# First attention of a two-layer kernel: keys laid out over all 128 partitions, one masked maximum for all scores, and two output strips begun before the attention ends

## The reference, cut to what matters

```python
# q (512 tokens, 8 heads, 64); k, v (512, 2 key heads, 64); k_ctx, v_ctx (256, 2, 64)
s_ctx = q . k_ctx * 64**-0.5            # all 256 context keys
s_loc = q . k     * 64**-0.5            # only keys with |i - j| <= 128
p = softmax(concat([sink, s_ctx, s_loc]))
att = p_ctx @ v_ctx + p_loc @ v         # four query heads share one key head
x = x + gate * (concat([att, conv]) @ w_out)
```

## Time and profile before

| | |
|---|---|
| median of 3 runs | 2669.1 us (2667.86 to 2671.85) |
| the profiled execution | 2669.28 us, its span 2667.3 us |
| PE busy | 2558.0 us (96%) |
| DVE busy | 1161.4 us (44%) |
| ACT busy | 752.9 us (28%) |
| TensorE clock granted, mean | 0.967 |
| first attention | 189.6 to 310.8 us |

### The profile page before, as it was taken

How to read it: one execution, slowest core, us unless ns; L and a number is a source line. 1 busy time by engine, 2 the same in 40 slices (tenths; PEclk the granted TensorE clock), 3 DMA queues, 4 the chain that set the end, 5 groups by cost and what they waited for, 6 DMA issues and landing times.

```text
span 2667.3 us, 29296 instructions
## 1 busy us (share of the span) xinstructions
PE 2558.0 (96%) x10842; PEld 1792.7 (67%) x10842; DVE 1161.4 (44%) x1793; ACT 752.9 (28%) x1052; POOL 29.4 (1%) x24
## 2 busy tenths in 40 slices
PE   6989969999999699999999999999999999999999
PEld 2765533333333488888988888888887566888887
DVE  5765351222221644443644443444435456544432
ACT  3124331000010423322433322333223435433321
POOL 0000000000000300000000000000000000000000
PEclk9986889999999799999899999999999999999999
DMA  6650138999999223331232322333322120323322
GB/s 243 199 188 1 55 151 345 422 422 421 422 422 377 79 88 101 101 109 59 88 95 97 108 98 83 95 98 98 113 92 76 59 72 9 95 95 97 108 98 75
DMA packets 80858, 403.58 MB, mean 151 GB/s; under 512 B 8984, under 2 KB 9496, under 8 KB 55968
## 3 DMA queue, kind: packets, MB, share of 16 engines
q1 hardware_dynamic: 80800, 402.82, 41.3%
HBM read 400.69 MB, written 2.10 MB: 151 GB/s over the span
## 4 chain that ended last, share of the span: by engine, by line
PE 88%; DVE 5%; DMA 2%; ACT 2%; issue 2%; POOL 0%; SPq 0%; DVEq 0%; ACTq 0%; POOLq 0%
PE pb L945 21%; PE pb L947 21%; PE pb L946 21%; PE pb L1150 8%; PE pb L1176 4%; PE pb L1137 2%; PE pb L1116 2%; DMA stage<-in_w_in 1%; PE pb L1038 1%; PE pb L1051 1%; PE pb L1065 1%; DMA adaw<-in_w_ada 1%; PE pb L1461 1%; PE pb L1331 1%; PE pb L1039 1%
## 5 line engine op out<-in xcount | busy, mean ns | idle before, releaser
L1485 DVE TENSOR_TENSOR wL<-stage,wH 128x1024 fp32r<-128x1024 f32 (+2 forms) x303 | 392.7, 1297 | 838.1 <-ACT wH L554 837.8
L945 PE MATMUL pb<-hH,wH 128*128 128x512 f32 x1688 | 668.7, 396 | 24.5 <-DVE gf L1847 8.5
L946 PE MATMUL pb<-hL,wH 128*128 128x512 f32 x1688 | 661.0, 392 | 0.0
L947 PE MATMUL pb<-hH,wL 128*128 128x512 f32 x1688 | 660.3, 391 | 0.0
L554 ACT ACTIVATE wH<-stage 128x1024 fp32r<-128x1024 f32 (+2 forms) x303 | 337.3, 1114 | 879.6 <-PE pb L947 809.5
L945 PEld LDWEIGHTS pb<-hH,wH 128*128 128x128 f32 x1688 | 319.3, 189 | 102.4 <-issue 12.5
L946 PEld LDWEIGHTS pb<-hL,wH 128*128 128x128 f32 x1688 | 319.2, 189 | 67.7 <-issue 2.7
L947 PEld LDWEIGHTS pb<-hH,wL 128*128 128x128 f32 x1688 | 319.1, 189 | 67.4
L945 PE MATMUL pb<-gH,wH 128*128 128x512 f32 x704 | 274.1, 389 | 0.0
L947 PE MATMUL pb<-gH,wL 128*128 128x512 f32 x704 | 274.1, 389 | 0.0
L946 PE MATMUL pb<-gL,wH 128*128 128x512 f32 x704 | 274.1, 389 | 0.0
(11 more groups left out here) (279 smaller groups left out, 2225.9 us busy)
## 6 DMA issues: line engine op xcount, KB each, us to landing
ring<-in_experts SPq DMA_DIRECT2D x192, 1024.0 KB, 17.5
stage<-in_gate SPq DMA_DIRECT2D x88, 512.0 KB, 3.5
stage<-in_up SPq DMA_DIRECT2D x88, 512.0 KB, 3.5
stage<-in_down SPq DMA_DIRECT2D x64, 704.0 KB, 4.0
adaw<-in_w_ada SPq DMA_DIRECT2D x48, 512.0 KB, 5.7
stage<-in_w_in SPq DMA_DIRECT2D x18, 512.0 KB, 6.7
stage<-in_mla_in SPq DMA_DIRECT2D x9, 512.0 KB, 3.4
stage<-in_q_up SPq DMA_DIRECT2D x12, 384.0 KB, 3.0
```

The costliest lines, as they stand in the source:

```text
L945: pe.matmul(ps, lh, rh, start=first, stop=False)
L946: pe.matmul(ps, lh, rl, start=False, stop=False)
L947: return pe.matmul(ps, ll, rh, start=False, stop=last)
L1485: dve.tensor_tensor(wL[:, n % 2, 0:w], stage[:, n % STAGE, 0:w], wH[:, n % 2, 0:w], ALU.subtract).then_inc(strip_lo, 1)
```

## The change

- `kZ` replaces the key tile: two tiles, one for each key head, of 128 rows; the head's own 64 rows hold its keys and context keys, the others zeros, written by POOL once the first conditioning sums are there. The scores are products over 128 rows of both query heads with one `kZ` tile.
- PSUM is named as four pairs of banks. A unit's context scores and the first 256 local ones fill the first bank of its pair, the last 128 of blocks 1 and 2 go to the second.
- One DVE instruction adds a mask to all 512 or 640 scores and takes the maximum. ACT's copy and DVE's first maximum are gone. The mask is longer and there is a second one for block 0; both are loaded before strip 6 of the input projection.
- The order on DVE within a unit is sink, mask and maximum, reciprocal of u-1, bias, scaling of u-1. ACT copies the fifth tile too, and does the copies of u-3 before the exponential of u. `LAG1` is 3.
- PE multiplies the convolution's half (k = 4 to 7) of output strips 0 and 1 between the last transposes, and the attention's half after `att_lo`.

```diff
@@ -115,7 +115,8 @@
     zero = np.zeros((P, P), np.float32)
-    window = np.concatenate([np.where(j >= i, 0, MASKED), zero, np.where(j <= i, 0, MASKED)], 1).astype(np.float32)
+    ahead, behind = np.where(j >= i, 0, MASKED), np.where(j <= i, 0, MASKED)
+    window = np.concatenate([zero, zero, ahead, zero, behind, zero, zero, zero, behind], 1).astype(np.float32)
@@ -185,12 +186,14 @@
         qT = place("qT", [P, 4, T], F32, G + 56 * KB)
-        kT = place("kT", [P, T + C], F32, G + 64 * KB)
+        kT = place("kT", [P, T], F32, G + 64 * KB)
+        kZ = place("kZ", [P, 2, T + C], F32, G + 48 * KB)
+        window_first = place("window_first", [P, C + 2 * P], F32, G + 54 * KB)
         vT = place("vT", [P, T + C], F32, G + 67 * KB)
         V = place("V", [P, 6, P], F32, G + 70 * KB)
         conv = place("conv", [P, 4, T], F32, G + 73 * KB)
         rope = place("rope", [P, 2, T], F32, G + 81 * KB)
-        window = place("window", [P, 3 * P], F32, G + 85 * KB)
+        window = place("window", [P, C + 3 * P], F32, G + 85 * KB)
@@ -245,7 +248,8 @@
         turns = place("turns", [P, T], F32, G + 80 * KB)
-        pb = [st.enter_context(nc.psum_tensor(f"pb{i}", [P, 512], F32)) for i in range(8)]
+        pair = [st.enter_context(nc.psum_tensor(f"pair{i}", [P, 1024], F32)) for i in range(4)]
+        pb = [pair[i // 2][:, 512 * (i % 2):512 * (i % 2) + 512] for i in range(8)]
@@ -381,7 +386,7 @@
         S2 = (6, 7, 0, 1)
-        LAG1, LAG = 2, 3
+        LAG1, LAG = 3, 3
@@ -448,8 +453,11 @@
             sp.dma_start(rope[:, :, :], A["rope"].rearrange("p (k t) -> p k t", k=2)).then_inc(small_loaded, 16)
-            sp.dma_start(window[:, :], A["window"]).then_inc(small_loaded, 16)
             for n in range(18):
+                if n == 6:
+                    sp.wait_ge(mod_summed, 2)
+                    sp.dma_start(window[:, :], A["window"][:, 0:C + 3 * P]).then_inc(window_loaded, 16)
+                    sp.dma_start(window_first[:, :], A["window"][:, C + 3 * P:2 * C + 5 * P]).then_inc(window_loaded, 16)
@@ -522,6 +530,9 @@
             pool.memset(eps[:, :], EPS).then_inc(ones_set, 1)
+            pool.wait_ge(mod_summed, 2)
+            pool.memset(kZ[64:128, 0, :], 0.0).then_inc(kz_cleared, 1)
+            pool.memset(kZ[0:64, 1, :], 0.0).then_inc(kz_cleared, 1)
@@ -680,15 +691,8 @@
                 act.activation(catH[:, 4 + k, :], conv[:, k, :], ACT.Copy).then_inc(cat_hi, 1)
-            def att_context(u):
-                if u >= 4:
-                    act.wait_ge(p_turned, u - 3)
-                act.wait_ge(scored, u + 1)
-                act.activation(prob[:, u % 4, 0:C], pb[2 * (u % 2) + 1][:, 0:C], ACT.Copy).then_inc(ctx_copied, 1)
-
             def att_exp(u):
                 lo_, hi_ = keys(UNITS[u][0])
-                act.wait_ge(ctx_copied, u + 1)
@@ -699,6 +703,8 @@
                     act.wait_ge(pv_done, n)
+                if len(kv_tiles[n]) == 5:
+                    act.activation(PT[:, j, 4, a * P:(a + 1) * P], pb[5][:, 0:P], ACT.Copy).then_inc(pt_fifth, 1)
@@ -708,12 +714,10 @@
             for u in range(len(UNITS) + LAG1 + 2):
-                if u < len(UNITS):
-                    att_context(u)
-                if 1 <= u <= len(UNITS):
-                    att_exp(u - 1)
                 if 0 <= u - LAG1 < len(UNITS):
                     att_turned(u - LAG1)
+                if u < len(UNITS):
+                    att_exp(u)
@@ -1031,29 +1035,31 @@
                     pe.wait_ge(rope_done, 5)
+                    pe.wait_ge(kz_cleared, 2)
                 else:
                     pe.wait_ge(masked, u - 1)
-                    pe.wait_ge(ctx_copied, u - 1)
-                q = qT[64 * j:64 * j + 64, a, n * P:(n + 1) * P]
-                pe.matmul(pb[2 * j][:, 0:hi_ - lo_], q, kT[64 * j:64 * j + 64, lo_:hi_], start=True, stop=True)
-                pe.matmul(pb[2 * j + 1][:, 0:C], q, kT[64 * j:64 * j + 64, T:T + C], start=True, stop=True).then_inc(scored, 1)
+                q = qT[:, a, n * P:(n + 1) * P]
+                pe.matmul(pb[2 * j][:, 0:C], q, kZ[:, j, T:T + C], start=True, stop=True)
+                mm = pe.matmul(pb[2 * j][:, C:2 * C], q, kZ[:, j, lo_:lo_ + C], start=True, stop=True)
+                if hi_ - lo_ > C:
+                    mm = pe.matmul(pb[2 * j + 1][:, 0:hi_ - lo_ - C], q, kZ[:, j, lo_ + C:hi_], start=True, stop=True)
+                mm.then_inc(scored, 1)
             def att_turn(u):
                 tiles = len(kv_tiles[UNITS[u][0]])
                 pe.wait_ge(p_ready, u + 1)
                 if u >= 2:
                     pe.wait_ge(pt_act, u - 1)
-                if tiles == 5:
-                    pe.wait_ge(v_ready, 2)
-                    pe.wait_ge(pt_dve, b_units(u))
                 for k in range(tiles):
+                    if k == 4:
+                        pe.wait_ge(v_ready, 2)
+                        pe.wait_ge(pt_fifth, b_units(u))
                     dst = pb[4 + 2 * (u % 2)][:, k * P:(k + 1) * P] if k < 4 else pb[5][:, 0:P]
                     mm = pe.transpose(dst, prob[:, u % 4, k * P:(k + 1) * P], tab("ident"))
                 mm.then_inc(p_turned, 1)
             def att_values(n):
                 pe.wait_ge(pt_act, 8 * n + 8)
-                pe.wait_ge(pt_dve, b_units(8 * n + 8))
@@ -1066,17 +1072,28 @@
                 mm.then_inc(pv_done, 1)
+            def mixed_out(s, features):
+
+                pe.wait_ge(strip_lo, W_OUT + s + 1)
+                pe.wait_ge(cat_lo, 4)
+                pe.wait_ge(masked, 31 + s)
+                for k in features:
+                    mm = three(pb[bank(T_OUT + s)][:, :], weights(W_OUT + s, k * P), (catH[:, k, :], catL[:, k, :]), k == 4, k == 3)
+                return mm
+
             for u in range(len(UNITS) + LAG1 + 1):
                 if u < len(UNITS):
                     att_scores(u)
                 if 0 <= u - LAG1 < len(UNITS):
                     att_turn(u - LAG1)
+                if 0 <= u - len(UNITS) < 2:
+                    mixed_out(u - len(UNITS), range(4, KD))
                 if block_at(u - LAG1 - 1) is not None:
                     att_values(block_at(u - LAG1 - 1))
-
-            pe.wait_ge(cat_lo, 4)
             pe.wait_ge(att_lo, NB)
-            for s in range(KD):
+            for s in range(2):
+                mixed_out(s, range(4)).then_inc(strip_used, 1)
+            for s in range(2, KD):
@@ -1588,7 +1605,11 @@
                 dve.wait_ge(rope_part, 2 * r0 + 2)
-                dve.tensor_tensor(dst, dst, tmp, ALU.add).then_inc(rope_done, 1)
+                if r0 == 0:
+                    dve.tensor_tensor(kZ[0:64, 0, 0:T], dst[0:64, :], tmp[0:64, :], ALU.add).then_inc(kz_ready, 1)
+                    dve.tensor_tensor(kZ[64:128, 1, 0:T], dst[64:128, :], tmp[64:128, :], ALU.add).then_inc(rope_done, 1)
+                else:
+                    dve.tensor_tensor(dst, dst, tmp, ALU.add).then_inc(rope_done, 1)
@@ -1600,7 +1621,12 @@
                     dve.tensor_copy(dst[:, 0:T], ps)
-                    dve.tensor_copy(dst[:, T:T + C], pb[bank(s) + 1][:, 0:C]).then_inc(out_taken, 1)
+                    if s == 0:
+                        dve.wait_ge(kz_cleared, 2)
+                        dve.tensor_copy(kZ[0:64, 0, T:T + C], pb[bank(s) + 1][0:64, 0:C])
+                        dve.tensor_copy(kZ[64:128, 1, T:T + C], pb[bank(s) + 1][64:128, 0:C]).then_inc(out_taken, 1)
+                    else:
+                        dve.tensor_copy(vT[:, T:T + C], pb[bank(s) + 1][:, 0:C]).then_inc(out_taken, 1)
@@ -1647,25 +1673,24 @@
                 n, a, j = UNITS[u]
-                w = keys(n)[1] - keys(n)[0]
-                off = P if n == 0 else 0
+                w = C + keys(n)[1] - keys(n)[0]
                 head = a + 4 * j
-                m1, m2 = stat[:, 28 + u % 4:29 + u % 4], stat[:, 32 + u % 4:33 + u % 4]
-                dve.wait_ge(ctx_copied, u + 1)
+                m2 = stat[:, 32 + u % 4:33 + u % 4]
                 if u >= 4:
                     dve.wait_ge(p_turned, u - 3)
-                dve.reduce_max(m1, prob[:, u % 4, 0:C], AX_X).then_inc(row_max, 1)
-                dve.tensor_copy(prob[:, u % 4, C + w:C + w + 1], stat[:, 48 + head:49 + head]).then_inc(row_max, 1)
+                else:
+                    dve.wait_ge(window_loaded, 32)
+                dve.tensor_copy(prob[:, u % 4, w:w + 1], stat[:, 48 + head:49 + head])
+                dve.wait_ge(scored, u + 1)
+                dve.tensor_tensor_reduce(prob[:, u % 4, 0:w], pair[j][:, 0:w], (window if n else window_first)[:, 0:w], 1.0, -3e38,
+                                         ALU.add, ALU.max, m2).then_inc(masked, 1)
                 if u:
                     invert_sum(u - 1)
-                dve.wait_ge(row_max, 2 * u + 2)
-                dve.tensor_tensor_reduce(prob[:, u % 4, C:C + w], pb[2 * j][:, 0:w], window[:, off:off + w], 1.0, m1,
-                                         ALU.add, ALU.max, m2).then_inc(masked, 1)
```

(26 more changed lines are left out.)

## The result

The changed kernel takes 2623.09 us (median of 4, 2622.03 to 2624.01) against 2668.48 us, a ratio of 0.9828 with the interval 0.9811 to 0.9845: 45 us less. The forecast was 2636, with 2626 to 2646 as its own range: the direction and the place were right, and the gain was sized too small by 12 us.

A forecast was written before the change was run, and what follows sets the result against it. PE was taken to bound the first attention at half clock, the round of ACT's copy, DVE's maxima and the fifth tile at full clock. 47.2 us gained less 3, 0.5, 2.4 and 8 left 33.3: 2636 us, range 2623 to 2656.

The forecast's parts named there:

- Scores at 0.43 and 0.22 a product, values at 3.6 and 4.5: First attention, full clock: 0.43 us per 256-column score product, 0.22 for 128 more; values 3.6 or 4.5 us a block.
- The first transposes at 196.3: Start of the first attention: 196.3 us instead of 196.65, the chain before shortened by one copy and one maximum only.
- Transposes, 12 x 0.59 + 16 x 0.74 = 18.9: First attention up to the last scores: transposes of 28 units, 0.59 us for four and 0.74 for five, 18.9 us.
- Joints, 2.4 us: First attention: PE idle between engines for 4% of its 60 us, 2.4 us off the gain, bounds 0 and 12.
- The clock in block 0, six units, 8 us: Block 0 of the first attention: clock 0.50 as before, six units costing 1.31 us more each, 8 us off the gain.
- The rule on transposes: First attention's clock: by the skill, transposes don't count as PE activity as products do, making alternating half clock likelier; no size.
- The tail, 13.7 us from the last scores to `att_lo`: End of the first attention, 255.4 to 269.1: transposes 2.4, strip halves 5.5, then 5.8 us at full clock.
- The gap before strip 2, 0.5: Output strips: strip 2 waits for strip 0, with 2.75 us covering some 3.2; 0.5 us lost, bounds 0 and 2.
- Input projection, 3 us: Before the attention: larger masks ahead of strip 6 cost 2.6 us, plus more DVE work; 3 us, bounds 0 and 5.
- patchwork: First attention: full clock after values, half later, 18 units at half costing 27 us instead of 8; 2655 us, chance 0.24.
- a pacing DVE: First attention: DVE waits for the exponential in every unit, 0.35 us each, 11 us more; 2647 us, chance 0.12.
- half clock throughout: First attention: half clock for the whole stage, 19 us slower than before, 2688 us; chance 0.06.

The follow-up runs named there:

- e2: Kernel before with only the zero-padded keys, scores over 128 rows, all else as before; 2647.53 us, ratio 0.9913.
- e9: Kernel before with padded keys used by block 0 only, 64-row scores in blocks 1 to 3; 2660.73 us, ratio 0.9968.
- e1: Changed kernel with scores multiplying only the 64 rows of their own key head; 2645.37 us, ratio to before 0.9906.
- e4: Changed kernel with the two masks loaded ahead of the first output strip instead of ahead of strip 6; 2622.39 us.
- e6: Changed kernel with masks loaded ahead of the output strips and the second early half strip split into the tail's two waits; 2621.84 us.
- e3: Changed kernel without the two early half strips, all eight output strips multiplied after att_lo; 2625.14 us.
- e8: Changed kernel with 128-row scores in block 0 only and 64-row ones in blocks 1 to 3; 2629.25 us, ratio 0.9852.

## Why the prediction was off, point by point

- *Scores at 0.43 and 0.22 a product, values at 3.6 and 4.5*: measured 0.44 and 0.22, 3.58 (208.52 to 212.10) and 4.44. Right.
- *The first transposes at 196.3*: measured 196.35, but by luck. The sum charged 3 us for the input projection on top, so it stood for 199.3, and **3.0 us** of the error lie here. The first score came 1.4 us later than before and not 3, and from there to the first transposes it took 5.3 us, where I had 6.7. I had taken off only a copy and a maximum; the table load that now runs beside DVE's work was not in the sum. Kernels with the old order take 7.0 us for this part (before, e2, e9), those with the new one 5.2 to 5.5, or 6.3 to 6.9 in the three profiled executions (e1, e4, e6) in which the clock stayed at half until about the first transposes or longer.
- *Transposes, 12 x 0.59 + 16 x 0.74 = 18.9*: mis-sized. They take 0.44 and 0.55, 14.1 in all: **4.8 us** of the error. The 0.59 was read from a place where a 64-row product follows; that transition is removed by the change, as e1 shows by bringing it back. Five were taken as 0.74 by the same measure.
- *Joints, 2.4 us*: from 196.35 to 253.95 there are 57.6 us. Scores 27.9, transposes 14.1 and values 12.5 make 54.5, so the joints are 3.1. Half of that, 1.6 us, are three waits for DVE's maximum (0.41, 0.41 and 0.73). In block 0 PE has no gap, but DVE's unit is 1.31 us as PE's is, so PE could not go much faster without meeting DVE.
- *The clock in block 0, six units, 8 us*: this step failed. I took "0.50 as before" from a stretch of 64-row scores although I had named the rows as what differs. The clock is up before the first transposes, and **8 us** were not lost. e1 has those 64 rows, and there block 0 does run at half clock until the values. The moment of the rise is not fixed: in e6, with the scores of the changed kernel, it comes at 198.9, after the first transposes at 197.26.
- *The rule on transposes* that I weighed from the Trainium skill ("TensorE: Matmul & The Clock Gate", PE-mode transpose) is not contradicted: 64-row scores between transposes did not raise the clock in 30 us of gapless work (e1). But with 128-row scores the transposes, a third of a unit's time, did no harm.
- *The tail, 13.7 us from the last scores to `att_lo`*: 13.8 (253.95 to 267.75). *The gap before strip 2, 0.5*: 0.51. Right. From `att_lo` to the norm it takes 4.6 us less than before (41.42 against 46.05), where the sum had 5.0. That the halves are worth little by themselves was in the sum, which adds them and takes them off again; e3 confirms it.
- *Input projection, 3 us*: 1.4 in this execution, and about 1.5 for the masks by the roundings of strips 3 to 7. Mis-sized by half.
- Not foreseen: routing gives back 1.0 us. From the norm to the first gather product it takes 39.6 us before and 40.6 now, and PE's first router products run at half clock for longer (from 316.15 to about 320.5, before from 364.11 to about 366.8).

The account, beginning with the forecast's 33.3: + 3.0 for the start, + 4.8 for the transposes, + 8 for the clock, - 0.7 for the joints, - 0.3 for scores, values and tail together, - 0.4 for the strips, - 1.0 for routing, which makes 46.7. The spans differ by 46.3; 0.4 us are lost behind the routing, and I did not look for their cause. The rivals: neither patchwork, nor a pacing DVE, nor half clock throughout took place.

## What to carry to other kernels

Where products over 64 rows alternate with transposes and the granted clock is 0.50 under a busy PE, pad the contraction to 128 rows with zeros: the product takes no longer, and here that alone gave 21 us of 2668. Removing PE's waits alone gave 23, and both together 45, so each pays without the other. A pitch read beside an operation that the change deletes is not the pitch afterwards: take it from a place with the new neighbour. Work used as filler belongs into the waits themselves, not ahead of them.

## What the runs showed of the hardware that I had not expected

- The same stream (64-row scores, transposes, no gaps) can run at either clock, by what came before it: at 0.50 in block 0 and at 1.00 after the first values (e1), and at 1.00 from the start of block 1 after a padded block 0 (e8).
- Changing between 64-row and 128-row weights costs PE time: 0.34 us of a 1.98 us unit (e1 against the changed kernel, both at 1.00).
- 128-row scores with zeros in half of the rows raised the clock from 0.50 to 1.00 (changed kernel, e2) and held it with PE busy for 12 of 15 us (e2). Other numbers of rows, or of zeros, were not tried.
